# Per-head norms: sums in four 32-column strips of TensorE, with the tokens along columns

## The reference

```
o    = rms_norm(o, g_rec_out) * silu(g)       # 4 heads of 128
attn = rms_norm(attn, g_attn_out)             # 8 heads of 64
mixed = concat(o, attn) @ w_out
rms_norm(x, g) = x * rsqrt(mean(x * x) + 1e-6) * g
```

## Time and profile before

| | us |
|---|---|
| median of 3 runs | 1689.72 |
| lowest, highest | 1678.05, 1700.59 |
| profiled execution | 1684.71 |
| its span | 1682.9 |
| TensorE busy (matmul) | 1628.8 (97%) |
| VectorE busy | 960.1 (57%) |
| ScalarE busy | 832.5 (49%) |
| GpSimd busy | 207.7 (12%) |
| granted clock, mean | 0.98 |

### The profile page before, as it was taken

How to read it: one execution, slowest core, us unless ns; L and a number is a source line. 1 busy time by engine, 2 the same in 40 slices (tenths; PEclk the granted TensorE clock), 3 DMA queues, 4 the chain that set the end, 5 groups by cost and what they waited for, 6 DMA issues and landing times.

```text
span 1682.9 us, 30109 instructions
## 1 busy us (share of the span) xinstructions
PE 1628.8 (97%) x12228; PEld 1539.5 (91%) x12228; DVE 960.1 (57%) x1581; ACT 832.5 (49%) x1480; POOL 207.7 (12%) x213
## 2 busy tenths in 40 slices
PE   6999999989999999999999999999899999999996
PEld 5998769988999999999899986799789999999995
DVE  6744436576446655435897444456844475553475
ACT  6426334347554755434664363344664556551552
POOL 3220102311000100000113102031200010000011
PEclk9999879999999999999999998999999999999998
DMA  6544542435344565434444465333534545562443
GB/s 200 191 143 155 189 163 91 135 103 166 103 151 154 162 186 183 130 102 149 149 144 135 127 222 175 123 125 102 169 101 129 163 151 173 183 189 82 134 153 107
DMA packets 77044, 247.82 MB, mean 147 GB/s; under 512 B 8771, under 2 KB 18243, under 8 KB 76780
## 3 DMA queue, kind: packets, MB, share of 16 engines
q1 hardware_dynamic: 76908, 245.90, 45.7%
HBM read 234.05 MB, written 14.44 MB: 148 GB/s over the span
## 4 chain that ended last, share of the span: by engine, by line
PE 87%; DVE 7%; DMA 2%; ACT 2%; issue 1%; SPq 0%; POOLq 0%; POOL 0%; DVEq 0%; ACTq 0%
PE ps L930 65%; PE ps L927 5%; PE ps L994 3%; DVE w_rest L1232 2%; PE ps L1178 1%; PE ps L1110 1%; PE ps L1123 1%; PE ps L1138 1%; DVE reg L1270 1%; DMA kc<-kcT 1%; PE ps L1153 1%; PE ps L1070 1%; DVE norm_every L1255 1%; DVE square_sum L1245 1%; DMA bias<-rel_scratch 1%
## 5 line engine op out<-in xcount | busy, mean ns | idle before, releaser
L930 PE MATMUL ps<-h_high,w_rest 128*128 128x320 f32 (+1 forms) x1920 | 580.6, 302 | 7.2 <-DVE h_rest L1290 6.2
L930 PE MATMUL ps<-h_rest,w_high 128*128 128x320 f32 (+1 forms) x1920 | 569.4, 297 | 0.0
L930 PE MATMUL ps<-h_high,w_high 128*128 128x320 f32 (+1 forms) x1920 | 569.3, 297 | 0.0
L681 ACT ACTIVATE w_high<-w_raw 128x1024 fp32r<-128x1024 f32 x384 | 402.1, 1051 | 234.9 <-PE ps L930 234.3
L1232 DVE TENSOR_TENSOR w_rest<-w_raw,w_high 128x1024 fp32r<-128x1024 f32 x380 | 481.3, 1271 | 64.6 <-ACT w_high L681 64.3
L930 PEld LDWEIGHTS ps<-h_high,w_rest 128*128 128x128 f32 x1920 | 365.3, 190 | 21.5 <-issue 17.0
L930 PEld LDWEIGHTS ps<-h_rest,w_high 128*128 128x128 f32 x1920 | 365.7, 190 | 0.5
L930 PEld LDWEIGHTS ps<-h_high,w_high 128*128 128x128 f32 x1920 | 365.4, 190 | 0.0
L930 PE MATMUL ps<-u_high,w_rest 128*128 128x320 f32 (+1 forms) x1024 | 306.0, 299 | 4.2 <-DVE u_rest L1330 3.2
L930 PE MATMUL ps<-u_rest,w_high 128*128 128x320 f32 (+1 forms) x1024 | 303.7, 297 | 0.0
L930 PE MATMUL ps<-u_high,w_high 128*128 128x320 f32 (+1 forms) x1024 | 303.6, 296 | 0.0
(11 more groups left out here) (174 smaller groups left out, 1810.6 us busy)
## 6 DMA issues: line engine op xcount, KB each, us to landing
w_raw<-w SPq DMA_DIRECT2D x384, 512.0 KB, 3.5
kc<-kcT SPq DMA_DIRECT2D x16, 512.0 KB, 7.7
vc<-vc SPq DMA_DIRECT2D x16, 512.0 KB, 6.4
s_in<-s SPq DMA_DIRECT2D x8, 512.0 KB, 6.9
ss<-s_in SPq DMA_DIRECT2D x8, 512.0 KB, 5.3
bias<-rel_scratch SPq DMA_DIRECT2D x8, 512.0 KB, 4.4
rel_scratch<-rel_row SPq DMA_DIRECT2D x1, 2560.0 KB, 12.4
bias<-rel_scratch SPq DMA_DIRECT2D x8, 256.0 KB, 5.1
```

The source lines that it names most:

```text
L681: A.activation(whi[:, v % RING], raw[:, v % RING], ACT.Copy).then_inc(S["w_hi"], 1)
L930: last = pe.matmul(ps[:, bank, 0:n], wt[:, slot, c, :], xt[:, c, :], **flags)
```

## The change

The sums keep the tokens along the columns. `r_sum` makes one matmul per head: 32 columns of ones are stationary, the squares move, and head a's sums come out on the 32 partitions from 32 a. `a_sum` does the same for pairs of heads with a constant `head_sum`, whose columns select one or the other head of the pair, and adds den^2 with eight more matmuls that transpose it (den squared stationary, the identity moving, two output partitions per strip). Root and reciprocal then work on the whole tile `head_norm` of 128 partitions and 320 or 256 columns. The spread is one matmul per head (K = 1 row of `head_norm` against a row of ones) or per pair of heads (K = 2 rows against `head_spread`). VectorE's den^2 moves one step ahead, to `a_sq`, with a semaphore of its own (a_den, in place of a_sum); its copy and its add are gone. The one tile is shared by both norms, so ScalarE waits for the spreads of the other norm before it writes the roots.

```diff
@@ -260,12 +260,13 @@
-    half = np.kron(np.eye(2), np.ones((DH, DH))).astype(np.float32)
     row = np.arange(P)
+    sums = (row[:, None] // DH == np.arange(32)[None] % 2)
+    spread = (row[:, None] % 32 == np.arange(P)[None] // DH)
-    cst = np.concatenate([eye, half, seq_of_tok, head_of_row, tok_of_row], 1).astype(np.float32)
+    cst = np.concatenate([eye, spread, seq_of_tok, head_of_row, tok_of_row, sums], 1).astype(np.float32)
...
@@ -335,7 +336,7 @@
-    cst = place("cst", [P, 288])
+    cst = place("cst", [P, 320])
@@ -347,18 +348,16 @@
-    den2 = place("den2", [P, 3 * HA])
-    root = place("root", [P, 3 * HA])
-    inv = place("inv", [P, 3 * HA])
-    r_root = place("r_root", [P, 3 * HR])
-    r_inv = place("r_inv", [P, 3 * HR])
+    den2 = place("den2", [P, 2 * HA])
+    rn = place("head_norm", [P, WIDE[0]])
-    half_ones = cst[:, P:2 * P]
+    head_spread = cst[:, P:2 * P]
+    head_sum = cst[:, 288:320]
...
@@ -799,10 +798,11 @@
             def r_sum(l, h):
+                n = WIDE[h]
                 act.wait_ge(S["r_ms"], 2 * l + h + 1)
-                if h == 0:
-                    A.activation(r_root[0:TS, 8:12], ps[0:TS, 2, 8:12], ACT.Sqrt, bias=eps[0:TS], scale=1.0 / P)
-                A.activation(r_root[:, 0:8], ps[:, 2, 0:8], ACT.Sqrt, bias=eps[:], scale=1.0 / P).then_inc(S["r_root"], 1)
+                if l or h:
+                    act.wait_ge(S["a_spr"], 8 * l + 4 * h)
+                A.activation(rn[:, 0:n], ps[:, 2, 0:n], ACT.Sqrt, bias=eps[:], scale=1.0 / P).then_inc(S["r_root"], 1)
@@ -861,10 +861,11 @@
             def a_sum(l, h):
-                act.wait_ge(S["a_sum"], 2 * l + h + 1)
+                act.wait_ge(S["a_ms"], 2 * l + h + 1)
+                act.wait_ge(S["r_spr"], 8 * l + 4 * h + 4)
                 if h == 0:
-                    A.activation(root[0:TS, 16:24], den2[0:TS, 16:24], ACT.Sqrt, bias=eps[0:TS], scale=1.0 / DH)
-                A.activation(root[:, 0:16], den2[:, 0:16], ACT.Sqrt, scale=1.0 / DH).then_inc(S["a_root"], 1)
+                    A.activation(rn[:, 0:TS], ps[:, 2, 0:TS], ACT.Sqrt, bias=eps[:], scale=1.0 / DH)
+                A.activation(rn[:, pro(h)], ps[:, 2, pro(h)], ACT.Sqrt, scale=1.0 / DH).then_inc(S["a_root"], 1)
@@ -1077,24 +1078,18 @@
             def r_sum(l, h):
                 pe.wait_ge(S["o_there"], 5 * l + (3 if h == 0 else 5))
                 take(2)
-                for t, (t0, rows) in enumerate(TILES[h]):
-                    for a in range(HR):
-                        o0 = 4 * t + a
-                        last = pe.matmul(ps[0:rows, 2, o0:o0 + 1], o_sq[h][:, a, t0:t0 + rows], ones[:, 0:1],
-                                         start=True, stop=True)
+                for a in range(HR):
+                    last = pe.matmul(ps[32 * a:32 * a + 32, 2, 0:WIDE[h]], ones[:, 0:32], o_sq[h][:, a, :], start=True, stop=True)
                 last.then_inc(S["r_ms"], 1)
                 held[2] = (S["r_root"], 2 * l + h + 1)
             def r_spr(l, h, g):
                 pe.wait_ge(S["r_inv"], 2 * l + h + 1)
+                take(3, 4)
                 for i in range(2):
                     a = 2 * g + i
-                    take(3 + i)
-                    for t, (t0, rows) in enumerate(TILES[h]):
-                        last = pe.matmul(ps[:, 3 + i, t0:t0 + rows],
-                                         r_inv[0:rows, 4 * t + a:4 * t + a + 1].broadcast_to([rows, P]),
-                                         ident[0:rows, 0:rows], start=True, stop=True)
-                    last.then_inc(S["r_spr"], 1)
+                    pe.matmul(ps[:, 3 + i, 0:WIDE[h]], ones[32 * a:32 * a + 1, :], rn[32 * a:32 * a + 1, 0:WIDE[h]],
+                              start=True, stop=True).then_inc(S["r_spr"], 1)
@@ -1191,26 +1186,27 @@
             def a_sum(l, h):
                 pe.wait_ge(S["a_sq"], 2 * l + h + 1)
+                pe.wait_ge(S["a_den"], 2 * l + h + 1)
                 take(2)
-                for t, (t0, rows) in enumerate(TILES[h]):
+                for j in range(HP):
+                    pe.matmul(ps[32 * j:32 * j + 32, 2, 0:WIDE[h]], head_sum, a_sq[h][:, j, :], start=True, stop=False,
+                              skip_group_check=True)
+                for c in range(2):
                     for j in range(HP):
-                        o0 = 8 * t + 2 * j
-                        last = pe.matmul(ps[0:rows, 2, o0:o0 + 2], a_sq[h][:, j, t0:t0 + rows], half_ones[:, 0:P:DH],
-                                         start=True, stop=True)
+                        c0 = HA * c + 2 * j
+                        last = pe.matmul(ps[32 * j:32 * j + 2, 2, pro(h, c)], den2[:, c0:c0 + 2], ident,
+                                         start=False, stop=(c == 1), skip_group_check=True)
                 last.then_inc(S["a_ms"], 1)
-                held[2] = (S["a_sum"], 2 * l + h + 1)
+                held[2] = (S["a_root"], 2 * l + h + 1)
             def a_spr(l, h, g):
                 pe.wait_ge(S["a_inv"], 2 * l + h + 1)
+                take(5, 6)
                 for i in range(2):
-                    take(5 + i)
-                    for t, (t0, rows) in enumerate(TILES[h]):
-                        for s in range(2):
-                            c = 8 * t + 2 * (2 * g + i) + s
-                            last = pe.matmul(ps[DH * s:DH * s + DH, 5 + i, t0:t0 + rows],
-                                             inv[0:rows, c:c + 1].broadcast_to([rows, DH]), ident[0:rows, 0:rows],
-                                             start=True, stop=True)
-                    last.then_inc(S["a_spr"], 1)
+                    j = 2 * g + i
+                    r = slice(32 * j, 32 * j + 2)
+                    pe.matmul(ps[:, 5 + i, 0:WIDE[h]], head_spread[r, :], rn[r, 0:WIDE[h]], start=True, stop=True)\
+                        .then_inc(S["a_spr"], 1)
                     held[5 + i] = (S["a_scaled"], 8 * l + 4 * h + 2 * g + i + 1)
@@ -1434,10 +1430,9 @@
             def r_sum(l, h):
+                n = WIDE[h]
                 dve.wait_ge(S["r_root"], 2 * l + h + 1)
-                if h == 0:
-                    V.reciprocal(r_inv[0:TS, 8:12], r_root[0:TS, 8:12])
-                V.reciprocal(r_inv[:, 0:8], r_root[:, 0:8]).then_inc(S["r_inv"], 1)
+                V.reciprocal(rn[:, 0:n], rn[:, 0:n]).then_inc(S["r_inv"], 1)
@@ -1513,18 +1508,16 @@
+            def a_sq_(l, h):
+                dve.wait_ge(S["p_exp"], unit(l, h, 7) + 1)
+                if l or h:
+                    dve.wait_ge(S["a_ms"], 2 * l + h)
+                V.scalar_tensor_tensor(den2[:], den[:], DH * EPS, den[:], ALU.mult, ALU.mult).then_inc(S["a_den"], 1)
             def a_sum(l, h):
-                dve.wait_ge(S["p_exp"], unit(l, h, 7) + 1)
-                own(V.scalar_tensor_tensor(den2[:, 0:16], den[:], DH * EPS, den[:], ALU.mult, ALU.mult))
-                dve.wait_ge(S["a_ms"], 2 * l + h + 1)
-                if h == 0:
-                    V.tensor_copy(den2[0:TS, 16:24], ps[0:TS, 2, 16:24])
-                own.wait()
-                V.tensor_tensor(den2[:, 0:16], den2[:, 0:16], ps[:, 2, 0:16], ALU.add).then_inc(S["a_sum"], 1)
+                n = WIDE[h]
                 dve.wait_ge(S["a_root"], 2 * l + h + 1)
-                if h == 0:
-                    V.reciprocal(inv[0:TS, 16:24], root[0:TS, 16:24])
-                V.reciprocal(inv[:, 0:16], root[:, 0:16]).then_inc(S["a_inv"], 1)
+                V.reciprocal(rn[:, 0:n], rn[:, 0:n]).then_inc(S["a_inv"], 1)
```

More of the change, by code:

```diff
@@ L403, in build @@
              "ss_done", "ss_max", "sp_exp", "sp_norm", "sp_t", "spt_there", "spv_done", "mo_set", "sel_done", "so_there",
-             "a_sq", "a_ms", "a_sum", "a_root", "a_inv", "a_spr", "a_scaled", "a_hi", "a_lo",
+             "a_sq", "a_den", "a_ms", "a_root", "a_inv", "a_spr", "a_scaled", "a_hi", "a_lo",
              "sq", "ssq", "n_ms", "n_root", "n_inv", "nap", "x_even", "x_odd", "h_hi", "h_even", "h_odd",
@@ L1549, in _ @@
                      "s_upd": s_upd, "r_sum": r_sum, "r_spr": r_spr, "q_big": q_big, "sc": sc_, "s_sc": s_sc, "s_div": s_div,
-                     "s_pv": s_pv, "a_sum": a_sum, "a_spr": a_spr}
+                     "s_pv": s_pv, "a_sq": a_sq_, "a_sum": a_sum, "a_spr": a_spr}
             late = []
```

## The result

| | before | after |
|---|---|---|
| median, us (19 runs each) | 1689.1 | 1677.2 |
| lowest, highest | 1678.1, 1700.6 | 1661.5, 1687.0 |
| ratio of the runs, 95% interval | | 0.991 (0.988 to 0.994) |
| span of the profiled execution | 1682.9 | 1676.4 |

The change makes the kernel 0.9% faster, 10.8 to 20.1 us by the interval. The 1687.0 us run of the changed kernel lies over 1.5% above its fastest and is left out of the ratio. The forecast was 1673, with 1658 to 1689 as its range. The two medians differ by 11.9 us and the two profiled spans by only 6.5, and most of what follows is about why neither is the number to explain.

A forecast was written before the change was run, and what follows sets the result against it. TensorE, busy 97% of the span with 87% of the chain, was taken as the bound. Terms -16.7 (TensorE work), -3.6 (clock), +3.6 (second-half chain) took 1684.7 to 1668.0; with 5.0 to the median, 1673 us, range 1658 to 1689.

The forecast's parts named there:

- Removed from TensorE: Old norm sums and spreads taken off TensorE in both halves: 20.3 us per layer.
- Added: New sums and spreads on TensorE, four strips taken as parallel: 10.1 us per layer.
- the other end: Rival that the strips run serially: 21.6 us per layer added on TensorE, 1692 to 1696 us, 8%.
- A: First half, recurrent sum to end of second attention spread: shorter sums and spreads, plus 1.78 us per layer from the clock.
- C: Second half, attention sum to end of the spreads: shorter sum and spreads, with root and reciprocal fitting in.
- The drain on a change of tiling mode: Rule that changing tiling mode drains TensorE: one tail more in each of 24 stretches would take 7.2 us of gain.
- The clock: First half, 512-column records behind the recurrent sum return to full clock: 1.78 us per layer, 3.6 us gained.
- B: Second half, recurrent sum to second score matmuls: longer reciprocal and root on the chain lose 1.78 us per layer.
- The chain in the second half: Second half's recurrent norm: reciprocal adds 1.57 us and root 0.21 on the chain, 1.78 per layer, 3.6 us lost.
- Hidden by 2.1 us: First half's attention reciprocal ends at 281.2, TensorE comes at 283.3; scan level work 2.2 us later, used two slots on.
- D: End of the first half's attention spreads to the norm's column sum (line 958, after 959): no loss forecast.
- Hidden by 0.6 us: First half's recurrent reciprocal ends at 248.1, TensorE comes at 248.7; rival that this cover is gone: 1680 us, 13%.

The follow-up runs named there:

- split: Changed kernel with the second half's recurrent norm alone back in its old form; ran only once, 1663.6 us.

## Why the prediction was right, and where it was not

The direction, the size and the range held. Point by point:

- **Removed from TensorE**: right, by rows. **Added**: sums 0.74 and 0.64 us where I said 0.81 and 0.71, spreads 0.81 and 0.70 where I said 0.81 and 0.71, attention sums 1.2 (0.75, then 0.62, overlapping) where I said 1.3. Taking four strips as parallel from rows of two was right; the full-width run puts the price of the other end at 4.4 us per layer in A alone.
- **A as a whole**: my terms give 1.62 + 2.32 + 1.1 + 1.92 + 1.78 = 8.7, measured 8.4. **C**: 1.4, measured 1.45.
- **The drain on a change of tiling mode**: the Trainium skill's rule (TensorEngine Tiling (Array Packing), Key Properties) agrees with the trace after all, and the price is small. The first record of the recurrent sum starts 0.12 us behind the last full-width record of the block ahead of it in the kernel before, 0.21 in the changed kernel, and 0.12 again in the run without strips. The old attention spreads, in two strips, already stood at 0.21. So an entry into strips costs 0.09 us, under a third of the tail that I had set for the rule. Stretch A has four new ones, 0.36 us, about the 0.3 that A missed. I had looked for the price in the tail of line 1153, and it lies at the start. What TensorE does in this time no run shows.
- **The clock**: the 3.6 us are there in stretch A (3.72 to 1.94 us, twice), but they are not a constant. Where the one-column sums stood ahead of the 512-column records, the clock fell behind them in 5 of 6 places (both layers of the kernel before, both with thin work added, one of two with the attention norm alone); where the dense sum stood there, in 16 places of eight profiled executions, it never did. So my estimate for the term is 5/6 of 3.6, about 3 us. Nor did the changed kernel get more clock: the mean over its runs is 0.976, as before. It spends the time at half clock in stretch B, where TensorE waits for others anyway. There it costs 0.2 us by the one comparison that the runs give: with the recurrent norm alone the clock was full in the whole of layer 1's B, which took 24.93 us, and half for some 3 us in layer 0's, which took 25.14. That is how A could gain 3.6 us at the same mean clock. The forecast had the gain and not the move.
- **The chain in the second half**: the mechanism was right, the term mis-sized. I said +1.78 per layer; it is +1.2, since VectorE's two weight remainders behind the reciprocal run in 2.29 instead of 2.98 us: GpSimd's pieces now lie beside the reciprocal, which they don't slow. I also put the wait in the wrong place. I said line 1123 (1118 in the changed kernel) would wait 3 us; it waits 0.4, and TensorE waits 2.1 us earlier, for h_rest.
- **"Hidden by 2.1 us"**, the first half's attention reciprocal: this step failed. TensorE's spread did not wait, as I said, but "it is used two slots on" was wrong for what stood behind it. D lost 1.3 and 1.4 us, where I had put nothing: 0.8 to 1.0 of it is this reciprocal, through VectorE's queue, then GpSimd's, to a level matmul four blocks later. What the rest is was not found. I had followed the reciprocal to its own reader and not to the readers of its neighbours in the queue.
- **Hidden by 0.6 us**, the first half's recurrent reciprocal: right. A stays at 41.05 with a short reciprocal.
- The 0.7 us behind layer 1's last spread was a cost that I had not put in. It comes with the changed kernel, its variants with thin work, short reciprocals or another order, and `split`; it comes neither with one norm alone nor without strips. It arises in one place, 358 us later, where a weight remainder on VectorE takes 1.90 us beside an addition on GpSimd, and 1.21 in the kernel before, where GpSimd's addition takes 3.99 instead of 1.06. Which of the two is held up differs; why was not tried.

With what the stretches show, the sum is -14.0 instead of -16.7: 2.7 us for D, 0.7 for A and 0.7 at the end against the forecast, 1.2 for B and 0.1 for C in its favour. So the errors cancelled in part, which was luck. 1689.1 - 14.0 = 1675 for the median. My 5 us between the profiled execution and the median were fair: with 19 runs the median of the kernel before lies 4.4 us above that execution.

## What to carry to other kernels

Follow an operation that gets longer on a side engine down three lists: its reader, whatever stands behind it in its own queue, and the queue of the engine that reads that. A cover of 2 us for the direct reader says nothing of the others, and reordering two steps of one block gave 0.5 of the 1.3 us back. Where runs spread by more than the change is worth, cut the trace into stretches between the same instructions and compare those; stretches of the same code then tell how large the noise is and where it lives. Compare whole runs at the same mean granted clock: that made a difference of 6 us visible which two medians of 12 and 29 runs had hidden.

## What the runs showed of the hardware

- Four matmuls of 32 output columns each, all on 128 rows, run side by side: 8 records of 320 columns in 0.74 us against 2.31 us on the full width. Matmuls of one or two rows in neighbouring row strips pair as well (four records in 0.81 us).
- Sixteen records whose stationary operand has two columns, in four strips, take 0.62 us, in one strip 1.91.
- The first record of a stretch in strips starts 0.21 us behind a full-width record, a full-width one 0.12.
- Behind matmuls of one column the clock fell in 5 of 6 places; behind the first half's sums with two moving columns in both layers of one kernel and in neither of another. Behind 2.3 us of dense work in the same place it did not fall in either of two.
- Between executions of one program the mean granted clock moved, and the span with it, by 15 us for 0.01.
- A subtraction of 128x1024 on VectorE takes 1.16 to 1.23 us while GpSimd is idle, 289 times out of 289; two of them beside GpSimd's subtraction took 2.78 and 2.98 us instead of 2.29. A reciprocal of 128x256 took 1.75 us with GpSimd beside it for 0.7 us and without.
